# Stick-breaking scores, logits and sums of block 2 moved into the retention loop, with two fixed banks for the late gates

## The reference, cut to what matters

```python
proj = rmsnorm(x, pre_g) @ w_in
y_ret = retention(ret_q, ret_k, ret_v) * silu(ret_g)        # 4 heads of 128
y_ssd = ssd_mixer(xbc, z, dt_raw, ...)                      # gated by silu(z) inside
y_sb  = stick_breaking(sb_q, sb_k, sb_v) * silu(sb_g)       # 4 heads of 128
y_mem = memory_read(mem_q, mem_n, w_mem_kv) * silu(mem_g)   # 4 heads of 128
y = concatenate([y_ret, y_ssd, y_sb, y_mem]) @ w_out
return x + rmsnorm(y, post_g)
```

```python
logits   = q @ k * d ** -0.5
log_1mb  = where(causal, log_sigmoid(-logits), 0)
tail     = reverse cumulative sum of log_1mb, without the element itself
w        = where(causal, exp(log_sigmoid(logits) + tail), 0)
y        = w @ v
```

## Time and profile before

| what | value |
|---|---|
| three runs | 1977.56, 1981.7, 1983.45 us |
| the profiled execution's own time | 1978.23 us |
| its span | 1976.3 us |
| PE busy | 1876.7 us, 95% |
| DVE busy | 1358.1 us, 69% |
| ACT busy | 913.2 us, 46% |
| mean granted TensorE clock | 0.99 |

### The profile page before, as it was taken

One profiled execution on the slowest core, in us unless ns is written; L12 is line 12 of the kernel. 1 busy time (PEld: TensorE's weight loads), 2 busy tenths in 40 slices (PEclk: granted clock), 3 DMA queues, 4 the chain that ended last, 5 costly groups with the idle time before them and its releaser, 6 DMA issues.

```text
span 1976.3 us, 29270 instructions
## 1 busy us (share of the span) xinstructions
PE 1876.7 (95%) x11406; PEld 1590.3 (80%) x11406; DVE 1358.1 (69%) x2421; ACT 913.2 (46%) x1603; POOL 27.8 (1%) x56
## 2 busy tenths in 40 slices
PE   7999999999999999999999989999999989999997
PEld 3777556688888888887756889999999879999886
DVE  6666675688788887765577566665767755767764
ACT  3345565543423231354565654444444643544552
POOL 0000000000000000000000000000000000000000
PEclk9999999999999999999999999999999999999998
DMA  7332201255354545323132454444454325554322
GB/s 290 126 107 68 120 27 60 97 163 183 103 220 176 209 182 202 143 85 101 53 145 68 146 189 169 171 173 157 163 162 138 96 97 171 162 160 141 106 86 97
DMA packets 55896, 272.21 MB, mean 138 GB/s; under 512 B 6352, under 2 KB 7504, under 8 KB 38608
## 3 DMA queue, kind: packets, MB, share of 16 engines
q1 hardware_dynamic: 48272, 225.40, 33.1%
q0 software_dynamic: 7488, 44.94, 6.5%
HBM read 269.27 MB, written 1.05 MB: 137 GB/s over the span
## 4 chain that ended last, share of the span: by engine, by line
PE 71%; DVE 13%; ACT 9%; issue 5%; DMA 1%; SPq 0%; ACTq 0%; DVEq 0%
PE bank L578 18%; PE bank L580 17%; PE bank L579 17%; ACT w_parts L1428 3%; PE bank L925 2%; DVE small_lo L1954 2%; PE bank L933 2%; PE bank L730 2%; PE bank L614 2%; DMA wide<-in_ada 1%; PE bank L1206 1%; PE bank L1208 1%; PE bank L1207 1%; PE bank L625 1%; PE bank L1022 1%
## 5 line engine op out<-in xcount | busy, mean ns | idle before, releaser
L578 PE MATMUL bank<-h_hi,small_hi 128*128 128x256 f32 (+3 forms) x992 | 312.1, 315 | 12.3 <-DVE small_lo L1954 6.2
L579 PE MATMUL bank<-h_lo,small_hi 128*128 128x256 f32 (+3 forms) x992 | 301.8, 304 | 0.0
L580 PE MATMUL bank<-h_hi,small_lo 128*128 128x256 f32 (+3 forms) x992 | 301.7, 304 | 0.0
L1954 DVE TENSOR_TENSOR small_lo<-ring,small_hi 128x1024 fp32r<-128x1024 f32 (+1 forms) x192 | 226.4, 1192 | 107.4 <-ACT small_hi L1426 105.9
L579 PE MATMUL bank<-h_parts,w_parts 128*128 128x256 f32 (+1 forms) x784 | 262.8, 335 | 0.0
L1957 DVE TENSOR_TENSOR w_parts<-ring,w_parts 128x2048 fp32r<-128x2048 f32 x87 | 199.3, 2291 | 91.9 <-ACT w_parts L1428 91.9
L1428 ACT ACTIVATE w_parts<-ring 128x2048 fp32r<-128x2048 f32 x86 | 164.0, 1907 | 176.1 <-PE bank L580 176.1
L578 PE MATMUL bank<-b_parts,w_parts 128*128 128x256 f32 (+1 forms) x656 | 218.8, 334 | 1.5 <-DVE w_parts L1957 1.1
L580 PE MATMUL bank<-b_parts,w_parts 128*128 128x256 f32 (+1 forms) x656 | 217.9, 332 | 0.0
L579 PE MATMUL bank<-b_parts,w_parts 128*128 128x256 f32 (+1 forms) x656 | 217.8, 332 | 0.0
L578 PEld LDWEIGHTS bank<-h_hi,small_hi 128*128 128x128 f32 (+2 forms) x992 | 187.8, 189 | 26.9 <-issue 13.9
(11 more groups left out here) (300 smaller groups left out, 3759.0 us busy)
## 6 DMA issues: line engine op xcount, KB each, us to landing
ring<-in_w SPq DMA_DIRECT2D x204, 512.0 KB, 3.5
ring<-in_w SPq DMA_DIRECT2D x96, 1024.0 KB, 4.8
lowrank<-in_rows POOLq DMA_DIRECT2D x24, 1024.0 KB, 5.1
prob<-in_rows POOLq DMA_DIRECT2D x24, 512.0 KB, 3.8
wide<-in_ada SPq DMA_DIRECT2D x8, 1024.0 KB, 9.9
ring<-in_w SPq DMA_DIRECT2D x14, 384.0 KB, 3.1
lowrank<-in_bias POOLq DMA_DIRECT2D x2, 2048.0 KB, 11.2
x<-in_x SPq DMA_DIRECT2D x2, 1024.0 KB, 9.9
```

The lines of the kernel that those rows point to most:

```text
L578: pe.matmul(ps, w[0][:, k, :], hi, start=k == 0, stop=False)
L579: pe.matmul(ps, w[0][:, k, :], lo, start=False, stop=False)
L580: return pe.matmul(ps, w[1][:, k, :], hi, start=False, stop=k == nk - 1)
L1954: dve.tensor_tensor(small_lo[:, slot, 0:size], small[:, slot, 0:size], small_hi[:, pair, 0:size].bitcast(F32), ALU.subtract).then_inc(*sig ...
```

## The change

Heads 0, 1 and 2 of stick-breaking get their scores at the end of retention rounds 0, 1 and 2 on PE, their logits at the end of rounds 1, 2 and 3 on DVE, and the ScalarE softplus at the end of rounds 1, 2 and 3 on ACT. DVE's `sb_softplus` of heads 0, 1, 2 stands in rounds 2, 3, 4. `sb_tail(0)` follows on PE in round 3, ahead of `ret_mean`. The work behind the loop is put in another order. All PE steps of the loop other than gates take their banks from `LATE_BANKS`, gates from the ninth on from `GATE_BANKS`, and so does the first tile of the output layer. `work` gets a fifth buffer: retention uses two of the five, stick-breaking four, and `sq` is divided likewise.

```diff
-        buffers("work", [work_all[:, W2 * i:W2 * i + W2] for i in range(4)])
+        buffers("work", [raw_all[:, a:a + W2] for a in (512, 512 + W2, 512 + 2 * W2, 512 + 3 * W2, 0)])
...
-    ps = next_bank("gate", l, i, until=("gated_in", "gate", l, i), among=GATE_BANKS if n > 11 else None)
+    ps = next_bank("gate", l, i, until=("gated_in", "gate", l, i), among=GATE_BANKS if n > 7 else None)
...
@@ PE, retention loop
                     mm = causal_product(ps, vals2["rv"][:, :, P * hd:P * hd + P], given("work", ("ret_decay", l, hd)))
                     full(mm, "retY", l, hd)
+                    if hd < 3:
+                        sb_scores(hd)
+                    else:
+                        sb_tail(0)
...
-                sb_scores(0)
-                sb_scores(1)
                 for hd in range(4):
                     ret_mean(hd)
+                sb_tail(1)
                 gate_tile(12)
-                sb_tail(0)
-                sb_tail(1)
-                sb_scores(2)
-                for hd in range(4):
+                for hd in range(2):
                     sum_squares(("ret", hd), l, 1, T, among=LATE_BANKS)
                 sb_scores(3)
+                sb_value(0)
+                for hd in range(2, 4):
+                    sum_squares(("ret", hd), l, 1, T, among=LATE_BANKS)
                 gate_tile(13)
-                sb_value(0)
...
-                    output_half(next_bank("out2", l, 0, until=("out_copied", l, 0)), 0, 0)
+                    output_half(next_bank("out2", l, 0, until=("out_copied", l, 0), among=GATE_BANKS), 0, 0)
...
@@ ACT, retention loop
                     high_y(4 + hd)
+                    if hd:
+                        sb_softplus(hd - 1)
                 gate_logistic(11)
...
-                sb_softplus(0)
-                sb_softplus(1)
+                sb_weight(0)
...
@@ DVE, retention loop
                         low_y(3 + hd)
+                    if hd > 1:
+                        sb_softplus(hd - 2)
+                    if 0 < hd < 4:
+                        sb_logit(hd - 1)
+                sb_tail(0)
+                for hd in range(4):
+                    ret_centre(hd)
+                sb_tail(1)
                 gate_split(12)
                 gate_silu(12)
-                sb_tail(0)
-                sb_logit(2)
-                sb_tail(1)
+                sb_logit(3)
                 gate_product(12)
-                for hd in range(4):
-                    ret_gated(hd)
-                sb_softplus(2)
-                sb_logit(3)
+                ret_gated(0)
+                ret_gated(1)
+                sb_gated(0)
+                ret_gated(2)
+                ret_gated(3)
+                sb_tail(2)
+                sb_softplus(3)
                 gate_split(13)
```

More of the change, by code:

```diff
@@ L1113, in ret_scores @@
                     pe.wait_ge(*event("roped", "rk", l, hd))
-                    causal_scores(("retS", l, hd), ("ret_decay", l, hd), heads2["rk"][:, hd, :], heads2["rq"][:, hd, :])
-                ret_scores(0)
-                for hd in range(4):
[L1118 to L1129, removed]
+                    causal_scores(("retS", l, hd), ("ret_decay", l, hd), heads2["rk"][:, hd, :], heads2["rq"][:, hd, :], LATE_BANKS)
                 def sb_scores(hd):
@@ L1328, in square @@
                     until = (*until, 1)
-                s = take(act, "sq", (name, l, k), until)
+                s = take(act, "sq", (name, l, k), until, among)
                 if kr:
@@ L1794, in _ @@
                         square(("ssd", g), l, k, 2, y2(4 + 2 * g + k))
[L1795 to L1802, removed]
                 def sb_softplus(hd):
-                    s = take(act, "sq", ("sb", l, hd), ("psum_full", "sbT", l, hd))
+                    s = take(act, "sq", ("sb", l, hd), ("psum_full", "sbT", l, hd), (0, 1))
                     s2 = given("sb_abs", (l, hd))
@@ L2640, in _ @@
                 ssd_y(3)
[L2641 to L2653, removed]
-                        gate_product(11)
-                    if hd:
-                        dve.wait_ge(*event("psum_full", "retY", l, hd - 1))
-                        dve.tensor_copy(y2(hd - 1), bank(("retY", l, hd - 1))[:, 0:T]).then_inc(*signal("ret_y", l, hd - 1))
-                        low_y(3 + hd)
                 def sb_logit(hd):
-                    z = take(dve, "work", ("sb_logit", l, hd), ("psum_full", "sbY", l, hd))[:, 0:W2]
+                    z = take(dve, "work", ("sb_logit", l, hd), ("psum_full", "sbY", l, hd), (2, 3, 4, 0))[:, 0:W2]
                     dve.wait_ge(*event("psum_full", "sbS", l, hd))
@@ L2695, in ret_gated @@
                     dve.tensor_tensor(y2(hd), y2(hd), gate[:, hd, :], ALU.mult).then_inc(*signal("gated", l, hd))
-                sb_logit(0)
-                sb_logit(1)
-                ret_centre(0)
-                ret_centre(1)
-                sb_softplus(0)
-                sb_softplus(1)
-                ret_centre(2)
-                ret_centre(3)
+                for hd in range(5):
+                    if hd < 4:
+                        e = take(dve, "work", ("ret_decay", l, hd), ("psum_full", "retY", l, hd), (0, 1))
+                        dve.wait_ge(*event("psum_full", "retS", l, hd))
+                        dve.tensor_tensor(e[:, 0:W2], bank(("retS", l, hd))[:, 0:W2],
+                                              c2("decay")[:, W2 * hd:W2 * hd + W2], ALU.mult).then_inc(*signal("ret_decay", l, hd))
+                        gate_split(8 + hd)
+                        gate_silu(8 + hd)
+                        for j in range(4 if hd == 0 else 0):
+                            dve.wait_ge(*event("rs", ("ssd", j // 2), l))
+                            dve.scalar_tensor_tensor(y2(4 + j), y2(4 + j), p2("ssd", lw)[:, j:j + 1],
+                                                     given("rs", (("ssd", j // 2), l))[:, 0:T], ALU.mult, ALU.mult).then_inc(*signal("gated", l, 4 + j))
+                    else:
+                        gate_product(11)
+                    if hd:
+                        dve.wait_ge(*event("psum_full", "retY", l, hd - 1))
+                        dve.tensor_copy(y2(hd - 1), bank(("retY", l, hd - 1))[:, 0:T]).then_inc(*signal("ret_y", l, hd - 1))
+                        low_y(3 + hd)
+                    if hd > 1:
+                        sb_softplus(hd - 2)
+                    if 0 < hd < 4:
+                        sb_logit(hd - 1)
@@ L2715, in _ @@
+                ret_gated(1)
[3 more added lines that the diff above has]
+                sb_tail(2)
+                sb_softplus(3)
                 gate_split(13)
                 gate_silu(13)
-                sb_gated(0)
-                sb_softplus(3)
-                sb_tail(2)
                 low_y(0)
```

43 lines of the change are left out of this document (30 added, 13 removed).

## The result

| | before | after |
|---|---|---|
| median, 5 runs each | 1982.83 us (1977.56 to 1984.99) | 1991.53 us (1990.03 to 1993.25) |
| ratio | | 1.0047, 95% interval 1.0032 to 1.0063 |
| span of the profiled execution | 1976.3 us | 1988.9 us |
| its mean granted clock | 0.990 | 0.986 |
| PE busy | 1876.7 us | 1883.1 us |

The change costs 8.7 us between the medians. The two profiled executions lie further apart, 12.6 us; a second profile of the kernel before, further down, shows why.

What follows compares the result with a forecast made beforehand. PE was taken as the bound, its waits set by other engines' order. Layer 2's 1.5 + 2.5 and layer 3's 5.3 + 0.5 gave +9.8 us: 1988.0 from the profile, 1991.5 from the median, forecast 1990, range 1983 to 1999.

Steps and rivals of the forecast that it cites:

- circle of DVE and ACT: Retention loop: DVE and ACT wait for each other, each round taking 6.8 us against about 4.9 us of PE work.
- first memory score, layer 2, without clock: Layer 2, behind the loop: first memory score at 1596.5 instead of 1593.95, +2.5 us.
- clock, layer 2: Behind layer 2's loop: granted clock falls to 0.50, costing 1.7 to 3.4 us, nearest 2.5.
- layer 3, last tail sum, without clock: End of layer 3's stick-breaking: DVE releases PE's `sb_tail(3)` at 1889.4, before at 1884.61.
- layer 3, last value, without clock: End of layer 3's stick-breaking: `sb_value(3)` at 1893.85 against 1888.48, +5.3 us.
- copied key, layer 3: Layer 3's start: first retention scores wait for ACT's copy out of the `memory_keys` bank, +0.65 us.
- Smaller signs: Expected trace signs, among them layer 3 waits of 2.5 us or more ahead of the last tail sum and last value.
- The output tile: Layer 2, output layer's first tile: 1.62 us bank wait goes, two 0.3 us waits come among memory heads, net −1.0 us.
- Clock in layer 3, +0.5 us: Behind layer 3's loop: lower clock comes, but some 2.4 us of slack ahead of 1889.4 take most of it.
- Layer 3's waits before: Kernel before, layer 3: same PE waits as layer 2, plus 1.99 us at the last tail sum and 0.44 us.
- the faster rival: Banks were the shortage and moved work fills DVE's idle time: −5 to −13 us, about 1970; chance 0.08.
- the slower rival: Lower clock twice in layer 3 through gates 14 and 15, and through layer 2's memory heads: +15, 1997; chance 0.12.

Runs made afterwards that it cites:

- a second profile of the kernel before: The kernel before, unchanged, run and profiled again: median 1982.68 us, profiled execution 1981.61 us at clock 0.987.
- with the clock kept: The changed kernel with matmuls of constants in PE's pauses ahead of `ret_mean(2)` and `ret_mean(3)`: 1988.71 us, ratio 1.0029.
- the first experiment: The kernel before with only the bank half of the change, all orders as before: 1979.95 us, ratio 0.9989.
- the first set: First of two sets of experiments, each with runs of the unchanged kernel before, whose medians were 1982.8 and 1983.2 us.

## Why the prediction was right, and where it was off

| step | predicted | measured |
|---|---|---|
| circle of DVE and ACT | 6.8 us | 6.79 us |
| last `ret_mean` after `memory_keys`, layer 2 | 1575.35 − 1541.05 = 34.30 us | 34.31 us |
| first memory score, layer 2, without clock | 52.90 + 2.5 = 55.4 us | 55.64 us with the clock kept, 0.6 of it overrun |
| clock, layer 2 | 2.5 us | 23.35 − 20.73 = 2.6 us |
| the same with clock | 57.9 us | 57.66 us |
| layer 3, last tail sum, without clock | 1889.4 − 1840.30 = 49.1 us | 49.23 us with the clock kept |
| layer 3, last value, without clock | 1893.85 − 1840.30 = 53.55 us | 53.74 us with the clock kept |
| copied key, layer 3 | +0.65 us | wait of 0.56 us |

*The circle.* Right in mechanism and size, and shown: moving one ACT instruction group ends it and the loss with it. The price of the wait came from walking both streams row by row; no busy share shows it, since DVE's and ACT's are as before, 68 and 46%. Smaller signs came out less well: the wait ahead of layer 3's last tail sum was to be 2.5 us or more and is 1.74.

*The output tile.* Net −1.0 us. Against the second profile of before, the way from the first memory score to layer 3 shortened by 247.8 − 246.7 = 1.1 us. The bank alone, in the kernel before, gave about 2 us.

*Clock in layer 2, +2.5 us: right in size, but its base was not.* It costs 2.6 us in the changed kernel. But the row on which the step rested, a full clock there in the first profile, isn't typical: in the second profile of before, 1.4 us are lost in the same place already (first memory score at 54.28 instead of 52.90 us), and another 1.5 us behind it, at 1629. The changed kernel has that second stretch too, from 1632 us on. So layer 2 grew by 2.3 us, not by 4.0: about 2.1 from the waits, 2.6 − 1.4 from the clock, −1.1 behind the first memory score.

*Clock in layer 3, +0.5 us: mis-sized, the step that failed.* I held that 2.4 us of slack ahead of the last tail sum would take most of it. The slack is PE's; but DVE, which sets that tail sum, itself waits for what PE computes at half clock. DVE of the changed kernel, layer 3, behind the last copy: it waits for gate 12, head 3's scores and `rs`.

```profile
1888.20 0.29 DVE L1911 TENSOR_SCALAR tmp<-tmp 128x256 f32<-128x256 f32 x1 [0.94 <-ACT tmp L1776]
...
1889.31 0.56 DVE L2645 TENSOR_SCALAR probT<-bank 128x384 f32<-128x384 f32 x1 [0.82 <-PE bank L1037]
...
1891.08 0.42 DVE L2677 TENSOR_TENSOR x<-x,rs 128x256 f32<-128x256 f32 x1 [0.28 <-ACT rs L1324]
```

And DVE in the run with the clock kept, where gate 12 is in time:

```profile
1886.11 0.56 DVE L2647 TENSOR_SCALAR probT<-bank 128x384 f32<-128x384 f32 x1 [0.42 <-PE bank L1037]
...
1887.87 0.42 DVE L2679 TENSOR_TENSOR x<-x,rs 128x256 f32<-128x256 f32 x1 [0.29 <-ACT rs L1326]
```

That is 2.04 us of waiting against 0.71, and the 1.3 us between them are nearly all of the 1.4 by which the tail sum came earlier with the clock kept. The prediction had 0.9 us here, all for `rms`; with the clock kept it was 0.7, of which 0.29 for `rms`. The step should have held 1.4 us at least; the 0.42 us for the scores may come from the overrun of the constants, so it can be more.

*Layer 3's waits before.* The prediction says that the same waits come in layer 3 as in layer 2. In the trace of before the two that it names there are 1.18 and 1.51 us instead of 2.24 and 1.04. The sum doesn't use them; the price of the faster rival does.

*The sum.* +9.8 us predicted, +9.3 us between the two like profiles and +8.7 us between the medians: 1.7 us too much in layer 2 and 1 us too little in layer 3 offset each other in part, and that the total came so close is to that extent luck. Of the slower rival one thing came: the lower clock came twice in layer 3 (1878 to 1886 and 1902 to 1906), but it was back at 1.00 from 1906 us on, ahead of the second memory score. The rival with the bank as the shortage fell with the first experiment; its grain of truth is the output tile. The Trainium skill (Perfetto Trace Analysis, "Identifying Performance Opportunities") reads a repeating gap as a possible want of SBUF or PSUM. Here another division of the banks was worth 0.1%, and the order of instructions on ACT decided the loss.

## What to carry to other kernels

Work placed in another engine's idle time is free only if its consumer isn't ahead of something that the first engine needs back: follow the data through both streams for one whole round, and compare the time after which the circle repeats with the bound engine's own work in a round (6.8 us against 4.9 here). Put the instruction that waits longest behind whatever it could hold up. Where a chain must wait, give PE independent work there, and read more than one profile of the base kernel before a term is built on a clock in it.

## What the runs showed of the hardware that was not expected

The same instructions with the same waits get a different clock from execution to execution. PE waits 2.24 us ahead of the stick-breaking scores in both profiles of before, and 2.3 us for a weight split in both (1627 and 1629 us); the clock fell to 0.50 behind each in one and in neither in the other. Each such stretch cost 1.4 to 1.5 us. Run times of one kernel follow it: in the runs of before with the first set, clocks of 0.989 went with 1978.7 to 1980.2 us and those of 0.986 with 1982.7 to 1986.0 us.

Filling a pause with idle matmuls paid, though they compute nothing: the first memory score of layer 2 came 2.0 us earlier and the last tail sum of layer 3 1.4 us, with 2.8 us between the medians of the changed kernel and of the one with 11 more matmuls per layer. Nine constants were a little too many: they held the last `ret_mean` back by 0.6 us.
